# A long convolution inside a two-layer kernel: another order on three engines, and GpSimd adding up the filter's magnitudes ahead of TensorE

## What is computed

```python
def hyena_filters(T, ...):
    filt = (hdn @ w4.astype(F32)).reshape(T, 2, D_INNER)
    filt = filt * jnp.exp(-t * deltas[None, :])[:, None, :]
    filt = filt / (jnp.sum(jnp.abs(filt), axis=(0, 1), keepdims=True) + HY_FILTER_EPS)
    return filt[:, 0], filt[:, 1]

def bidir_long_conv(v, h_fwd, h_bwd, skip):
    y = jnp.fft.irfft(jnp.fft.rfft(vf, n=n, axis=1) * jnp.fft.rfft(taps, n=n, axis=0)[None],
                      n=n, axis=1)[:, :T]
    return (y + vf * skip.astype(F32)).astype(v.dtype)
```

## Time and profile before

| | |
|---|---|
| median of 3 runs | 2404.24 us (2402.88 to 2405.18) |
| the profiled execution, its time | 2406.78 us |
| the profiled execution, its span | 2405.0 us |
| PE busy | 2236.0 us, 93% |
| DVE, ACT, POOL busy | 57%, 42%, 26% |
| eight blocks of the convolution | about 415 to 715 us of the span |

### The profile page before, as it was taken

The page is one execution under the profiler, slowest core; times in us unless marked ns, Lnnn a source line. Parts: engine busy times, 40 slices in busy tenths (PEclk is TensorE's granted clock), DMA queues, the critical chain, the costliest instruction groups (busy, mean ns, idle before and its releaser), DMA issues.

```text
span 2405.0 us, 36878 instructions
## 1 busy us (share of the span) xinstructions
PE 2236.0 (93%) x15305; PEld 1855.4 (77%) x15305; DVE 1367.0 (57%) x2335; ACT 1004.5 (42%) x1832; POOL 618.4 (26%) x520
## 2 busy tenths in 40 slices
PE   7999999898999989999999989889989999699998
PEld 7999999888999989899999867856776677333332
DVE  4455546788872566666666667789455664411112
ACT  4344334444432455655656553435433432211112
POOL 1111123555541132322323201203220111133331
PEclk9999999899999999999999989999988999799999
DMA  5322332110014223222222224312331143799993
GB/s 182 103 74 88 101 116 79 44 36 19 32 54 135 62 69 82 71 74 78 72 69 80 54 53 102 103 36 75 86 113 49 32 126 116 268 367 376 371 377 145
DMA packets 226337, 274.78 MB, mean 114 GB/s; under 512 B 41192, under 2 KB 193737, under 8 KB 213626
## 3 DMA queue, kind: packets, MB, share of 16 engines
q1 hardware_dynamic: 210330, 256.68, 33.4%
q0 software_dynamic: 15264, 13.65, 1.8%
q10 hardware_dynamic: 576, 2.10, 0.2%
HBM read 305.18 MB, written 23.13 MB: 137 GB/s over the span
## 4 chain that ended last, share of the span: by engine, by line
PE 67%; DVE 17%; ACT 8%; issue 4%; DMA 2%; POOL 1%; SPq 0%; DVEq 0%; POOLq 0%; ACTq 0%
PE ps L93 15%; PE ps L94 14%; PE ps L95 14%; PE ps L4073 7%; PE ps L4116 4%; PE ps L1884 2%; ACT sp L115 2%; ACT whi L99 1%; DVE wlo L103 1%; DVE prods L1198 1%; PE ps L3189 1%; DVE fsum L1021 1%; PE ps L4043 1%; PE ps L3056 1%; DVE p L2182 1%
## 5 line engine op out<-in xcount | busy, mean ns | idle before, releaser
L93 PE MATMUL ps<-hn_h,whi 128*128 128x264 f32 (+2 forms) x2256 | 690.9, 306 | 26.7 <-DVE wlo L103 7.7
L95 PE MATMUL ps<-hn_h,wlo 128*128 128x264 f32 (+2 forms) x2256 | 672.9, 298 | 0.0
L94 PE MATMUL ps<-hn_l,whi 128*128 128x264 f32 (+2 forms) x2256 | 672.5, 298 | 0.0
L93 PEld LDWEIGHTS ps<-hn_h,whi 128*128 128x128 f32 x2256 | 431.4, 191 | 51.9 <-issue 18.2
L94 PEld LDWEIGHTS ps<-hn_l,whi 128*128 128x128 f32 x2256 | 431.6, 191 | 9.5 <-issue 0.2
L95 PEld LDWEIGHTS ps<-hn_h,wlo 128*128 128x128 f32 x2256 | 430.0, 191 | 11.5
L103 POOL TENSOR_TENSOR wlo<-wraw,whi 128x2048 fp32r<-128x2048 f32 (+1 forms) x44 | 158.3, 3598 | 464.0 <-ACT whi L99 464.0
L99 ACT ACTIVATE whi<-wraw 128x2048 fp32r<-128x2048 f32 (+1 forms) x134 | 202.4, 1511 | 43.9 <-PE ps L95 37.4
L103 DVE TENSOR_TENSOR wlo<-wraw,whi 128x2048 fp32r<-128x2048 f32 (+1 forms) x90 | 172.7, 1919 | 50.3 <-ACT whi L99 50.1
L4073 PE MATMUL ps<-ex_raw,xT 128*64 128x512 f32 x600 | 135.5, 596 | 0.0
L766 DVE SCALAR_TENSOR_TENSOR c<-ub,vec,c 128x528 f32<-128x528 f32 x48 | 45.6, 949 | 122.5 <-ACT c L115 122.5
(11 more groups left out here) (704 smaller groups left out, 5312.0 us busy)
## 6 DMA issues: line engine op xcount, KB each, us to landing
ex_raw<-in_w_gate_up SPq DMA_DIRECT2D x49, 1024.0 KB, 8.0
wraw<-in_hy_w_in SPq DMA_DIRECT2D x32, 1024.0 KB, 5.6
wraw<-in_da_w_in SPq DMA_DIRECT2D x64, 512.0 KB, 4.3
ex_raw<-in_w_down SPq DMA_DIRECT2D x26, 1024.0 KB, 7.5
wraw<-in_w_gate_up SPq DMA_DIRECT2D x15, 1024.0 KB, 7.5
wraw<-in_w_in SPq DMA_DIRECT2D x14, 1024.0 KB, 5.5
wraw<-in_hy_w_out SPq DMA_DIRECT2D x8, 1024.0 KB, 7.6
wraw<-in_da_w_out SPq DMA_DIRECT2D x8, 1024.0 KB, 8.2
```

What stands on the lines that cost most here:

```text
L93: e.matmul(out, lhsT=l[0], rhs=r[0], start=start, stop=False)
L94: e.matmul(out, lhsT=l[0], rhs=r[1], start=False, stop=False)
L95: return e.matmul(out, lhsT=l[1], rhs=r[0], start=False, stop=stop)
```

## The change

Four edits, all in the convolution:

1. `gpsimd_total`, new, on GpSimd: it adds the magnitudes of tile 1 to those of tile 0 (128x512), then the second half to the first (128x256). It stands at z = 4 ahead of the low part of z = 4. `tensor_filter_end` now waits for it and for `ab` of tile 2, and issues one matmul with ones and two with `once` for each half: 12 passes for 24.
2. `tensor_filter_end` of block c + 1 moves from behind both `tensor_back_end` to between `tensor_back` of half 0 and of half 1.
3. ScalarE copies `hc` of z + 1 ahead of the `Y_h` of z.
4. On VectorE, `vector_freq` moves ahead of `fsum` at z = 1 and 3, `vector_larger` ahead of the next `hp`; at z = 4 `fsum` of tile 2 moves behind `vT_l` and `vector_larger`, and the weights `w4s` behind that. Those of block 1 move ahead of the first block.

```diff
+    def gpsimd_total(e, w, c):
+
+        w.wait_ge("cv.vec", "ab", c, 1)
+        a, b = (dec[:, i].rearrange("p s c -> p (s c)") for i in range(2))
+        e.tensor_tensor(a, a, b, ALU.add).then_inc(*mark("cv.pool", "both", c))
+        w.wait_ge("cv.pool", "both", c)
+        e.tensor_tensor(dec[:, 0, 0], dec[:, 0, 0], dec[:, 0, 1], ALU.add).then_inc(*mark("cv.pool", "total", c))
+
     def tensor_filter_end(e, w, c):
...
+        w.wait_ge("cv.pool", "total", c)
+        w.wait_ge("cv.vec", "ab", c, 2)
         for h in range(2):
-            for i in range(3):
-                w.wait_ge("cv.vec", "ab", c, i)
-                for s in range(2):
-                    t = e.matmul(vb[0][:, h:h + 1], lhsT=dec[:, i, s, 128 * h:128 * h + 128], rhs=once if i == 2 else ones[:, 0:1],
-                                 start=(i == 0 and s == 0), stop=(i == 2 and s == 1))
+            cols = slice(128 * h, 128 * h + 128)
+            e.matmul(vb[0][:, h:h + 1], lhsT=dec[:, 0, 0, cols], rhs=ones[:, 0:1], start=True, stop=False)
+            for s in range(2):
+                t = e.matmul(vb[0][:, h:h + 1], lhsT=dec[:, 2, s, cols], rhs=once, start=False, stop=s == 1)
         t.then_inc(*mark("cv.pe", "norm", c))
@@ tensor_conv
             tensor_back(e, w, c, 0)
+            if c < 7:
+                tensor_filter_end(e, w, c + 1)
             tensor_back(e, w, c, 1)
             tensor_back_end(e, w, c, 0)
             tensor_back_end(e, w, c, 1)
-            if c < 7:
-                tensor_filter_end(e, w, c + 1)
@@ scalar_conv
         for c in range(8):
+            scalar_freq(e, w, c, 0)
             for z in range(5):
-                if c + z == 0:
-                    scalar_freq(e, w, 0, 0)
                 if c < 7:
                     scalar_filter(e, w, c + 1, z if z < 4 else 5)
-                if c + z:
-                    scalar_freq(e, w, c, z)
-                if c < 7 and z == 4:
+                if z < 4:
+                    scalar_freq(e, w, c, z + 1)
+                elif c < 7:
                     scalar_turned(e, w, c + 1)
...
                 scalar_product(e, w, c, z)
@@ vector_conv
                 if c < 7:
                     vector_filter(e, w, n, z if z < 4 else 5)
-                    if z in (1, 3):
-                        vector_differ(e, w, n, z // 2)
+                vector_freq(e, w, c, z)
+                if c < 7 and z in (1, 3):
+                    vector_differ(e, w, n, z // 2)
+                    vector_larger(e, w, n, z // 2)
                     if z == 3:
                         vector_filter(e, w, n, 4)
-                    elif z == 4:
-                        vector_differ(e, w, n, 2)
-                if c + z:
-                    vector_freq(e, w, c, z)
-                if c < 7 and z in (1, 3):
-                    vector_larger(e, w, n, z // 2)
...
+            if c < 7:
+                vector_turned(e, w, n)
+                vector_larger(e, w, n, 2)
+                vector_differ(e, w, n, 2)
             if c < 6:
                 vector_w4(e, w, c + 2)
             if c < 7:
-                vector_turned(e, w, n)
-                vector_larger(e, w, n, 2)
                 vector_sums(e, w, n, 0)
                 vector_sums(e, w, n, 1)
@@ gpsimd_conv
         for c in range(8):
             for z in range(5):
+                if c < 7 and z == 4:
+                    gpsimd_total(e, w, c + 1)
                 gpsimd_freq(e, w, c, z)
```

More of the change, by code:

```diff
@@ L1332, in scalar_conv @@
         scalar_unit(e, w, (7, 3, 1), hy_step[7, 3, 1])
+        scalar_w4(e, w, 1)
         scalar_sums(e, w, 0)
-        scalar_w4(e, w, 1)
         for c in range(8):
+            scalar_freq(e, w, c, 0)
             for z in range(5):
-                if c + z == 0:
-                    scalar_freq(e, w, 0, 0)
                 if c < 7:
                     scalar_filter(e, w, c + 1, z if z < 4 else 5)
-                if c + z:
-                    scalar_freq(e, w, c, z)
-                if c < 7 and z == 4:
+                if z < 4:
+                    scalar_freq(e, w, c, z + 1)
+                elif c < 7:
                     scalar_turned(e, w, c + 1)
-                elif c == 7 and z == 2:
+                if c == 7 and z == 2:
                     filters_over(w)
@@ L1380, in vector_head @@
             vector_differ(e, w, 0, 2)
+            vector_w4(e, w, 1)
             vector_larger(e, w, 0, 2)
@@ L1386, in vector_conv @@
         vector_unit(e, w, (7, 3, 1))
-        vector_w4(e, w, 1)
         for c in range(8):
@@ L1390, in vector_conv @@
             for z in range(5):
-                if c + z == 0:
-                    vector_freq(e, w, 0, 0)
                 if c < 7:
                     vector_filter(e, w, n, z if z < 4 else 5)
-                    if z in (1, 3):
-                        vector_differ(e, w, n, z // 2)
+                vector_freq(e, w, c, z)
+                if c < 7 and z in (1, 3):
+                    vector_differ(e, w, n, z // 2)
+                    vector_larger(e, w, n, z // 2)
                     if z == 3:
                         vector_filter(e, w, n, 4)
-                    elif z == 4:
-                        vector_differ(e, w, n, 2)
-                if c + z:
-                    vector_freq(e, w, c, z)
-                if c < 7 and z in (1, 3):
-                    vector_larger(e, w, n, z // 2)
                 elif c == 0 and z == 0:
@@ L1453, in gpsimd_conv @@
         e.dma_start(lb_x[:], C["lb"]).then_inc(*land("left"))
+        gpsimd_total(e, w, 0)
         gpsimd_w4(e, w, 1)
```

## The result

The changed kernel takes 2470.28 us (2468.24 to 2474.69, four runs) beside 2403.56 us of the kernel before: a ratio of 1.028, 95% interval 1.0262 to 1.0297. It is slower by 67 us. I had forecast 2439 us with a range to 2453, so the sign was right and the size, 35 us for 67, about half. The profiled execution took 2468.24 us with a span of 2466.5.

The account below looks back on a forecast made before the run. PE, busy for 93% of the span, was taken to bound the kernel. Waits 28, GpSimd 5.6, clock 5.6 and first block -4 gave +35 us: forecast 2439 us, range 2421 to 2453.

Parts of the forecast that it names:

- The chain to the last magnitudes: Block's end: `ab` of tile 2 comes 6.9 us after freq of z = 4; PE waits, +4.0 us per block.
- GpSimd's additions in VectorE's way: At z = 4: the additions hold up `rr` in the chain to `ab`, 0.8 us per block, +5.6 us.
- The halved passes: Block's end: halving saves PE 1.35 us per block, but at the old place it turns into waiting for `y0`.
- The clock: Half 1 and the ends: half clock after PE's standing, 0 to 1.65 us per block, booked 0.8, +5.6 us.
- Rival 2: Convolution: GpSimd catches `rr` at z = 1 and 2 too, slow stretch per tail; about +52 us, chance 0.17.
- The loop: Over z: `prods` wait goes, `hp` wait grows; nothing booked, range -1 to +1.5 us per block.
- The first block: First block: early `w4s` removes the wait for `w4`'s low part and `hp` comes sooner, booked -4 us.

Follow-up runs that it names:

- a2_only_up: The kernel before with only the passes, all 24, moved up between the two halves of the back transform: 2453.63 us, ratio 1.0213.
- a1_end_place: The changed kernel with the passes put back behind both ends of the back transform: 2448.35 us, ratio 1.017 to the kernel before.
- a4_only_orders: The kernel before with only the new orders of ScalarE and VectorE and block 1's early weights: 2444.38 us, ratio 1.0155.
- a3_only_total: The kernel before with only GpSimd's additions and the twelve passes, at the old place: 2411.76 us, ratio 1.0026.
- b1_fill_tail: The changed kernel with 28 unused matmuls per block between half 0 and the passes: 2444.41 us, ratio 1.0159 to the kernel before.
- b4_only_dve: The kernel before with only VectorE's new order and its early weights of block 1: 2444.07 us, ratio 1.0163.
- c1_first_block: The kernel before with only block 1's weights early and `hp` ahead of `prods` at c = 0, z = 0: 2400.47 us, ratio 0.9985.

## Why the prediction was wrong

**The chain to the last magnitudes: right.** Forecast 6.9 us from the freq of z = 4 to `ab` of tile 2, and 0.8 for GpSimd. The chain's first link in the changed kernel:

```profile
542.97 0.69 ACT L115 ACTIVATE hc<-ps,wf 57x512 f32<-57x512 f32 x1 [9.44 <-PE ps L1172]
```

From there to the end of `dec`, 549.66 + 0.82 = 550.48, it is 7.5 us, beside 6.9 and 0.8. The wait at the passes is 4.03 us and the one for `y0` 1.00, where I had about 3.6 with 0.8 to come, and 1.2. `a2_only_up` shows that the move brings a wait and a loss by itself, and `a1_end_place` that the late chain is paid at the old place too, as a wait for `y0`.

**GpSimd's additions in VectorE's way: right in kind and near in size.** Forecast 0.8 us a block, by a hit on `rr` of z = 4. The second `rr` of z = 4 took 0.94 us for 0.42, so 0.52 in the chain. The `dec` of tile 2 took 0.82 for 0.67, but that isn't the additions' doing: in `a4_only_orders`, which has none, it takes 0.89 to 0.91. With the old order, in `a3_only_total`, they catch the two `fsum` in place of `rr`, for 1.6 us, and cost 8 us in seven blocks.

**The halved passes: right that they bring nothing.** Their 1.35 us were cover for `y0`; `a3_only_total` shows the wait that replaces it.

**The clock: this is the step that failed.** "Between 0 and 1.65 us per block; I take the middle, 0.8". The upper bound itself was too low, for it allowed one stretch of 3.4 us like the one before, worth 1.65. What came is 10.2 us from inside the wait to the end of half 1. `b1_fill_tail` measures its cost: 3.5 us per block, 1.2 on the passes and 2.3 on half 1. I had added the passes at the full-clock price, from a row at the full clock, in a place that they would reach after 4 us of standing. Rival 2, "everything in full", named this mechanism with its sign and was too cheap by the same bound.

**The loop: booked at nothing, and it was not.** From the signal to the back transform a block is 47.9 - (560.66 - 542.77) = 30.0 us long, for 38.2 - 9.6 = 28.6 before: +1.4, at the edge of my -1 to +1.5. The wait for `prods` went, as forecast. The wait for the `hp` of tile 2 was put at 2.3 and is 2.91. That for the `hp` of tile 1 was put at 0 to 0.4 and is 2.25. The rows of VectorE at z = 1 show what makes it late:

```profile
523.04 0.89 DVE L1213 TENSOR_TENSOR rr<-prods 128x256 f32<-128x256 f32 x1
523.85 1.54 DVE L1214 TENSOR_TENSOR rr<-prods 128x256 f32<-128x256 f32 x1
...
526.97 1.75 DVE L1027 TENSOR_TENSOR dec<-dec,sq 128x512 f32<-128x512 f32 x1
```

Beside them GpSimd works at low parts and the fold:

```profile
522.34 1.30 POOL L103 TENSOR_TENSOR Y_l<-rr,Y_h 128x512 fp32r<-128x512 f32 x1 [1.94 <-ACT Y_h L99]
523.61 1.50 POOL L103 TENSOR_TENSOR yl<-gg,yh 128x528 fp32r<-128x528 f32 x1
...
526.78 1.39 POOL L103 TENSOR_TENSOR Y_l<-rr,Y_h 128x512 fp32r<-128x512 f32 x1 [1.67 <-ACT Y_h L99]
```

Three instructions of 0.42, 0.42 and 0.67 us take 4.18 us where they would take 1.5: 2.7 us, of a kind that I had given to rival 2 alone, and there at 1 us a block. The rule of the Trainium skill that I weighed for the additions ("SBUF — State Buffer", Who interferes with whom) bears on these too, and the trace agrees: the second `rr` ends at 525.39, after `yl`, whose row ends at 525.11. I had applied it to the instructions that are new, and not to those that had moved beside old ones. That these catches are what the 2.25 us consist of is read from the rows; no run takes GpSimd out of their way. `b4_only_dve` has the same wait, 2.22 us, with both `rr` at 0.42, and there an `fsum` (1.79) and the `dec` (1.22) are caught.

**The first block: right for the kernel before, less in the changed one.** Forecast -4 us, and `c1_first_block` measures -3.9. In the changed kernel the first back transform starts 2.8 us sooner (446.81 for 449.61). There GpSimd's additions for block 0 catch the early `w4s`, two instructions that take 1.94 and 0.94 us for 0.43 and 0.42 in `c1_first_block`, and the passes of block 0 wait 1.96 us for the `dec` behind them. I had booked the additions at z = 4 and not here.

**The account.** Forecast per block 4.0 + 0.8 + 0.8 = 5.6; measured 9.7. The difference of 4.1 is 2.7 us of clock (3.5 for 0.8) and 1.4 us of loop. The two traces differ by 2466.5 - 2405.0 = 61.5 us, 26 more than the 35 that I had booked. Six blocks, from the first signal behind a back transform to the last, bring 25 of them. The first of these signals starts at 464.86 for 459.21, 5.7 us later where I had 1.6: the first tail is 18.05 us long for 9.6, dearer by 2.8 than booked, and the early gain is 2.8 for 4. Behind the last signal 2.8 us come back. The medians lie 5 us further apart than the two traces.

The parts alone cost 50, 8 and 41 us, 99 in sum, and 67 together. They share waits and slow stretches, so no part's price is its own.

## What to carry to other kernels

Before work is moved up on an engine that runs in order, look when its last operand is ready in the profile of before: here 3.5 us after the new place, with nothing else changed. Price a long wait on TensorE as the wait plus what stands behind it at the half clock. In the changed kernel the half clock came with all seven waits of 4.0 us at the passes and with all five of 2.9 in the loop, but with only one of six of 2.2; in `b4_only_dve` it came with those of 2.2 as well, so the length of one wait doesn't decide it. Count small work in its old place for what it covers. When an order is changed, check every pair of VectorE and GpSimd instructions that come to lie side by side, not only the new ones.

## What was not expected of the hardware

- Work that nobody uses made the kernel faster: 28 matmuls of 266 columns in a 4 us wait took the block from 47.9 to 44.4 us.
- One-column passes take twice as long at the half clock: twelve took 2.56 us, and 1.33 us at the full clock.
- In the changed kernel the half clock held for 10.2 us at a stretch, over 34 matmuls of PE, although 22 of them were full-width ones in a row behind the passes. I had no row before with more than 3.4 us in a settled block. The Trainium skill's "TensorE: Matmul & The Clock Gate", Part 1, has the throttled clock as the default, released by activity. The trace agrees in kind on the fall: the clock fell inside the wait in which PE stood for 4.03 us, and with the wait filled it stayed at 1.00. On the release it shows how late that can come: PE was busy again from 550.63, and the clock was back only at 558.2, 7.6 us on.
